# A feed-forward down projection by seven products of halves, with part of its side work on GpSimd and ScalarE and the residual's scale inside the down stage

## The chip, the cores and the metric

The kernel runs on one core of one Trainium2 chip. The metric is the device time of one execution in microseconds (us); the time before is the median of three runs, 1853.4 us (1850.56 to 1854.05).

## The reference

One decoder layer in float32 with 1024 tokens, D_MODEL = 1024 and D_FF = 2816. Two attention branches give h; then comes the feed-forward part, whose last product is what the change is about:

```python
h = _layernorm(alpha * x + attention_branches(x), ...)
ug = _causal_conv3(h @ w_up, conv)          # (1024, 2 * 2816), gate half and value half
f = silu(ug[..., :2816]) * ug[..., 2816:]   # (1024, 2816)
out = _layernorm(alpha * h + f @ w_down, ln2_g, ln2_b)   # w_down is (2816, 1024)
```

(The helper names of these lines are shortened here; the shapes and the order are the reference's.)

## The kernel before

**Precision.** Every float32 operand of TensorE is kept as a high part (a copy rounded to the format that TensorE takes at full pace) and a low part (operand minus high part). A product of a 128-row block is three matmuls, high x high, low x high, high x low, which `split3` issues (L1055, L1056, L1057). So each operand costs one copy (ScalarE or GpSimd) and one subtraction (VectorE or GpSimd), and TensorE gets three matmuls of 128 x 512.

**Engines and order.** The program is one straight instruction list per engine, written by hand; semaphores join them. SyncE (SP) issues most of the transfers, ScalarE a few. An engine that waits holds up all that stands behind it in its list, SP's transfers too.

**The up stage** computes the transposed u = (h @ w_up), two f row blocks (a pair) at a time, so there are 11 pairs. The four halves of a pair's weights and of h are multiplied by a seven-product scheme (Strassen's, in Winograd's form): seven products of halves in place of eight, at the price of sums of the operands and of the results. There are two such sets for a pair (gate and value blocks), 14 products of 12 matmuls each. Their weights pass through a ring of 8 slots: ScalarE makes the high part (`up_high`, L2777) when TensorE has freed the slot, GpSimd the low part (`up_low`, L990), and some weight sums on the way. When a pair's products are done, ScalarE reads banks back: copies of a bank into `p_sb` (L2810, L2816), the first tap of the convolution for the gate (`gate_id`, L2826, into `up_g`) and for the value, and silu. VectorE adds the other taps (L2130, L2135) and multiplies silu(gate) by the value in `value_conv` (L2153), which leaves f in `up_g`: two row blocks, each in two halves of 512 tokens. SP stores each half to `d_f` in DRAM as soon as `f_ok` counts it (`f_store`, L787). `gate_id` of the next pair overwrites `up_g`, and so waits until the stores have landed (`f_out`).

**The down stage** computes tokens x D_MODEL: `down(i, t)` for 22 weight slots i (11 for each half of the output's columns), 8 token tiles t, two row blocks of f and three matmuls each, 6 matmuls of 128 x 512 a call into one of eight banks. f comes back from DRAM in row blocks of 1024 tokens (`f_load`, L790, eight buffers `f_raw`); ScalarE makes the high part (`f_high`, L2927), VectorE the low part (`f_low`, L1576), and each f block is fetched and split twice, once for each column half. Weights: GpSimd makes both parts in one pass each (L928, L930). The rows of h for the residual are fetched whole by ScalarE's queue (L2981) into `z_tok`, VectorE applies the first layer norm's gain and bias to them, and alpha enters when a bank is evicted (`scalar_tensor_tensor` of z_tok, alpha and the bank, L2250). Then the second layer norm follows row by row: statistics on VectorE, the scaling on ScalarE, the gain on VectorE (L2256), the bias on GpSimd (L1043), the stores on SP (L841) and ScalarE.

## Time and the profile before

| | before |
|---|---|
| three runs, median | 1853.4 us |
| profiled execution | 1850.84 us |
| its span | 1849.0 us |
| TensorE matmuls busy | 1783.6 us (96%) |
| TensorE weight loads busy | 1484.4 us (80%) |
| VectorE busy | 906.2 us (49%) |
| ScalarE busy | 719.3 us (39%) |
| GpSimd busy | 917.0 us (50%) |
| granted TensorE clock | 0.993 of full |
| HBM read, written | 159.14 MB, 58.74 MB |

The profiled execution is one run with the profiler on; its span runs from the first to the last recorded instruction. Records of matmuls overlap, so the mean length of a record isn't the time that one matmul adds; a count over a stretch gives that. Busy shares are means over stages with different limits.

### The profile page before, as it was taken

The page shows a single profiled execution, that of the slowest core. Times are in us where ns is not written, and L with a number is a line of the kernel's source. Part 1 is how long each engine was busy: PE and PEld are TensorE (multiplying, and loading weights), DVE is VectorE, ACT ScalarE, POOL GpSimd, SP SyncE. Part 2 cuts the span into 40 slices and gives each one's busy share as a digit, 9 for nine tenths or more (in the row PEclk, how much of TensorE's full clock was granted, in tenths as well). Part 3 has the DMA queues.
Part 4 walks back from the last instruction along what each step waited for, and adds up shares of the span by engine and source line. Part 5 has one row for each costly group of instructions (what it writes and reads, how often), then busy time and mean ns, then how long its engine had stood idle before and what let it go on. Part 6 is the DMA issues. An engine that isn't in the chain of part 4 may idle for free.

```text
span 1849.0 us, 23075 instructions
## 1 busy us (share of the span) xinstructions
PE 1783.6 (96%) x8596; PEld 1484.4 (80%) x8596; DVE 906.2 (49%) x1515; ACT 719.3 (39%) x1295; POOL 917.0 (50%) x718
## 2 busy tenths in 40 slices
PE   8999999999999999999989999999999999999996
PEld 6788887888888777888867888778888888788884
DVE  6213312535444475545455535655455554656447
ACT  6434434333433224545451113744444544211222
POOL 6788754211212542323323375777677766343343
PEclk9999999999999999999999999999999999999998
DMA  5434324213122569223334343223222322754432
GB/s 171 122 103 125 108 88 149 72 55 86 52 92 69 165 208 299 87 80 97 97 114 141 133 182 132 74 85 99 83 77 73 99 80 70 265 190 169 160 103 91
DMA packets 202525, 219.39 MB, mean 119 GB/s; under 512 B 22381, under 2 KB 145437, under 8 KB 202413
## 3 DMA queue, kind: packets, MB, share of 16 engines
q1 hardware_dynamic: 164350, 144.76, 25.3%
q10 hardware_dynamic: 38064, 73.15, 11.2%
q8 instruction: 70, 1.15, 0.3%
q14 instruction: 41, 0.34, 0.1%
HBM read 159.14 MB, written 58.74 MB: 118 GB/s over the span
## 4 chain that ended last, share of the span: by engine, by line
PE 85%; DVE 5%; POOL 3%; ACT 2%; DMA 2%; issue 2%; SPq 1%; ACTq 0%; DVEq 0%; POOLq 0%
PE psum_all L1055 24%; PE psum_all L1057 24%; PE psum_all L1056 24%; PE psum_all L1376 1%; PE psum_all L1392 1%; PE psum_all L1394 1%; PE psum_all L1393 1%; DMA ga_st<-d_sga 1%; DVE pT_lo L1576 1%; PE psum_all L1119 1%; PE psum_all L1123 1%; POOL xs L867 1%; PE psum_all L1090 1%; PE psum_all L1121 1%; PE psum_all L1364 1%
## 5 line engine op out<-in xcount | busy, mean ns | idle before, releaser
L928 POOL CAST w_hi<-w_raw 128x512 fp32r<-128x512 f32 (+4 forms) x104 | 93.1, 895 | 495.2 <-PE psum_all L1057 462.4
L930 POOL TENSOR_TENSOR w_lo<-w_raw,w_hi 128x512 fp32r<-128x512 f32 (+4 forms) x104 | 213.2, 2050 | 8.5
L1055 PE MATMUL psum_all<-xT_hi,w_hi 128*128 128x512 f32 (+1 forms) x456 | 182.3, 400 | 7.5 <-POOL w_lo L864 3.3
L1057 PE MATMUL psum_all<-xT_hi,w_lo 128*128 128x512 f32 (+1 forms) x456 | 179.1, 393 | 0.0
L1056 PE MATMUL psum_all<-xT_lo,w_hi 128*128 128x512 f32 (+1 forms) x456 | 179.1, 393 | 0.0
L1055 PE MATMUL psum_all<-t_hi,w_hi 128*128 128x512 f32 x352 | 137.3, 390 | 2.8 <-DVE psum_all L2190 2.3
L1057 PE MATMUL psum_all<-t_hi,w_lo 128*128 128x512 f32 x352 | 137.0, 389 | 0.0
L1056 PE MATMUL psum_all<-t_lo,w_hi 128*128 128x512 f32 x352 | 137.0, 389 | 0.0
L990 POOL TENSOR_TENSOR w_lo<-s_sb,w_hi 128x512 fp32r<-128x512 f32 x88 | 112.8, 1294 | 43.9 <-ACT w_hi L2777 43.9
L944 POOL TENSOR_SCALAR p_sb<-p_sb,small 128x128 f32<-128x128 f32 (+3 forms) x64 | 48.0, 751 | 171.6 <-DVE small L1954 171.5
L990 POOL TENSOR_TENSOR w_lo<-w_raw,w_hi 128x512 fp32r<-128x512 f32 x66 | 84.8, 1287 | 57.9 <-ACT w_hi L2777 57.7
L1055 PEld LDWEIGHTS psum_all<-xT_hi,w_hi 128*128 128x128 f32 (+1 forms) x456 | 86.5, 190 | 29.2 <-DVE xr L1588 3.5
L1055 PE MATMUL psum_all<-b_hi,w_hi 128*128 128x512 f32 x264 | 104.2, 395 | 3.2 <-ACT p_sb L2810 3.2
L1056 PE MATMUL psum_all<-b_lo,w_hi 128*128 128x512 f32 x264 | 103.9, 394 | 0.0
L1057 PE MATMUL psum_all<-b_hi,w_lo 128*128 128x512 f32 x264 | 103.8, 393 | 0.0
L1057 PEld LDWEIGHTS psum_all<-xT_hi,w_lo 128*128 128x128 f32 (+1 forms) x456 | 86.0, 189 | 19.3
L1056 PEld LDWEIGHTS psum_all<-xT_lo,w_hi 128*128 128x128 f32 (+1 forms) x456 | 86.1, 189 | 17.8
L864 POOL TENSOR_TENSOR w_lo<-w_raw,w_hi 128x512 fp32r<-128x512 f32 x56 | 73.1, 1313 | 44.9 <-ACT w_hi L2289 44.9
L1055 PE MATMUL psum_all<-x_h,w_hi 128*128 128x512 f32 x224 | 87.4, 390 | 1.6 <-POOL w_lo L864 0.8
L1682 DVE TENSOR_TENSOR xp<-psum_all,xp 128x512 f32<-128x512 f32 x14 | 9.7, 690 | 160.8 <-PE psum_all L1057 160.8
L1057 PE MATMUL psum_all<-x_h,w_lo 128*128 128x512 f32 x224 | 87.2, 389 | 0.0
L1056 PE MATMUL psum_all<-x_l,w_hi 128*128 128x512 f32 x224 | 87.2, 389 | 0.0
(536 smaller groups left out, 4873.0 us busy)
## 6 DMA issues: line engine op xcount, KB each, us to landing
w_raw<-in_w_up_dram SPq DMA_DIRECT2D x44, 512.0 KB, 4.1
f_raw<-d_f SPq DMA_DIRECT2D x44, 512.0 KB, 3.5
w_raw<-in_w_in_dram SPq DMA_DIRECT2D x36, 512.0 KB, 4.7
d_f<-up_g SPq DMA_DIRECT2D x44, 256.0 KB, 3.2
w_raw<-in_w_down_dram SPq DMA_DIRECT2D x22, 512.0 KB, 4.5
w_raw<-in_w_out_dram SPq DMA_DIRECT2D x8, 1024.0 KB, 5.1
x_tok<-in_x_dram SPq DMA_DIRECT2D x8, 512.0 KB, 6.7
d_sga<-x_st ACTq DMA_DIRECT2D x16, 256.0 KB, 2.0
```

The source lines that it names most:

```text
L864: nc.gpsimd.tensor_tensor(x_ring(g, True), x_operand(g), x_ring(g).bitcast(F32), ALU.subtract).then_inc(sm["up_w"], 1)
L867: nc.gpsimd.tensor_tensor(dst, a, b, op).then_inc(sm["s_ok"], 1)
L928: wc.done(nc.gpsimd.tensor_copy(w_hi[b][:, w], src[:, w]))
L930: low = nc.gpsimd.tensor_tensor(w_lo[b][:, w], src[:, w], w_hi[b][:, w].bitcast(F32), ALU.subtract)
L944: nc.gpsimd.tensor_scalar(p_sb[s % 3][:, 0:wp], p_sb[s % 3][:, 0:wp], prec[:, s % 2:s % 2 + 1], 1.0, ALU.mult, ALU.mult).then_inc(sm["p_no ...
L990: nc.gpsimd.tensor_tensor(ring(g, True), operand(g), ring(g).bitcast(F32), ALU.subtract).then_inc(sm["up_w"], 1)
L1055: pe.matmul(out_ap, ah, bh, start=start and i == 0, stop=False, skip_group_check=more)
L1056: pe.matmul(out_ap, ah, bl, start=False, stop=False, skip_group_check=more)
L1057: last = pe.matmul(out_ap, al, bh, start=False, stop=stop and i == len(terms) - 1, skip_group_check=more)
L1090: last = pe.transpose(bank(kind)[:, i * P:(i + 1) * P], s_ap, ident[:, :])
L1119: pe.matmul(psum[5][:, 0:DV], att[i % 2][:, :], v_tok[:, t, :], start=True, stop=t == 0)
L1121: pe.matmul(psum[5][:, 0:DV], q_all[h % 2][:, t, 0:2, :], state[:, :], start=False, stop=True)
```

## The change

The down stage takes the seven-product scheme too. f is cut into blocks by row block (even or odd one of a pair) and by token half, w_down likewise by row block and by column half (`NEAR`, `FAR`). There are 77 steps g, seven products p of 11 steps m; a step multiplies one f tile of 128 x 512 (four token tiles) by one weight tile of 128 x 512, three matmuls for each token tile.

- **f and its sums.** After a pair's last f half, VectorE forms three sums of the pair's four f halves, and replaces one half by a difference (`f_sums`). SP then stores seven tiles (`f_store`), after all of the sums. The down stage fetches one tile of 128 x 512 a step (`fa_load`, five buffers), so that each is fetched once.
- **Weights.** The whole of w_down is fetched as four blocks of 2816 KB, one of them in two transfers, and stays in SBUF: one block before the end of the up stage, two at its end, the last ahead of the f tile of step 10. The high parts come from ScalarE (`wd_high`), the low parts from GpSimd (`up_low`), through the ring of the up stage. Three of the four weight sums are on VectorE ("t1", "t2", "t4" in `dn_sums`), one on GpSimd.
- **Results.** ScalarE copies the first product's banks to three places of z each and the fourth's to one (`first_rows`); VectorE adds the others (`evict`). Where products share a bank, the matmuls accumulate in it.
- **Residual.** SP fetches half rows of h into two buffers (`h_load`), two steps ahead of their use; VectorE applies gain and bias and adds alpha times the row to z ("h" in `dn_sums`), in steps 24 to 26, 31 to 39 and 54 to 57.
- **End.** The last six steps are done token tile by token tile. In the last layer norm GpSimd now multiplies by the gain as well as adding the bias for the first four rows, and adds the bias for two more.

```diff
-        d_f = dram("d_f", [FT, P, S])
+        d_f = dram("d_f", [7, FT // 2, P, HALF])
...
+        for m in range(NK):
+            dn_at(7 + m // 2, "t1", m)
+        for m in range(NK):
+            dn_at(10 + m if m < 2 else 12 + m, "t2", m)
+        for j in range(16):
+            dn_at(24 + j if j < 3 else 28 + j if j < 12 else 42 + j, "h", j)
+        for t in range(4):
+            dn_at(27 + t, "S2", t)
+            dn_at(49 + t, "S3", t)
+            dn_at(60 + t, "S1", t)
+        for m in range(NK):
+            dn_at(42 + m, "t4", m)
...
-                sp.dma_start(d_f[2 * m + u, :, half * HALF:(half + 1) * HALF], up_g[u][half][:, :]).then_inc(f_out[u], 16)
...
+            def f_store(m):
+                sp.wait_ge(sm["f_sums"], m + 1)
+                for what, src, landed in (("A11", up_g[0][0], f_out[0]), ("S3", up_g[0][1], f_out[0]), ("A12", up_g[1][0], f_out[1]),
+                                          ("A22", up_g[1][1], f_out[1]), ("S1", f_sum[0], s_out), ("S2", f_sum[1], s_out), ("S4", f_sum[2], s_out)):
+                    sp.dma_start(d_f[DN.index(what), m], src[:, :]).then_inc(landed, 16)
...
+            def fa_load(g):
+                if g >= AR:
+                    sp.wait_ge(sm["fs_lo"], g - AR + 1)
+                p, m = divmod(g, NK)
+                sp.dma_start(fa_raw[g % AR][:, :], d_f[p, m]).then_inc(tile_in[g % AR], 16)
+
+            def h_load(j):
+                if j >= 2:
+                    sp.wait_ge(*dn_sum("h", j - 2))
+                t, c = H_ROWS[j]
+                sp.dma_start(hr[j % 2][:, :], d_h[t * P:(t + 1) * P, c]).then_inc(hr_in[j % 2], 16)
...
-                    for u in range(2):
-                        for half in range(2):
-                            f_store(m - 1, u, half)
+                    f_store(m - 1)
...
+            for g in range(AR):
+                fa_load(g)
+            sp.wait_ge(sm["up_mm"], DN0)
+            sp.dma_start(wd_all[1][:, :, :], wdq[0][:, :, FAR]).then_inc(wd12_in[0], 16)
+            sp.dma_start(wd_all[3][:, :, :], wdq[1][:, 0:8, FAR]).then_inc(wd22_in[0], 16)
+            sp.dma_start(wd_all[4][:, :, :], wdq[1][:, 8:NK, FAR]).then_inc(wd22_in[0], 16)
+            for g in range(AR, DN_STEPS):
+                if g == 8:
+                    f_store(PAIRS - 1)
+                if g == NK - 1:
                     for u in range(2):
-                        for half in (1, 0):
-                            f_store(PAIRS - 1, u, half)
...
+                        sp.wait_ge(f_out[u], 32 * PAIRS)
+                    sp.wait_ge(s_out, s_out_from + 48 * PAIRS)
+                    sp.dma_start(wd_all[2][:, :, :], wdq[1][:, :, NEAR]).then_inc(wd21_in[0], 16)
+                    sp.wait_ge(sm["h_stored"], 16 * TT)
+                fa_load(g)
+                for j in range(16):
+                    if ("h", j) in DN_AT.get(g + 2, ()):
+                        h_load(j)
...
+            for g in range(DN_STEPS):
+                up_low(PRODUCTS + g)
+                if 13 <= g <= 33 and g % 2:
+                    m = (g - 13) // 2
+                    pool.wait_ge(*wd22_in)
+                    pool.wait_ge(*dn_sum("t1", m))
+                    w_sum(wd12[m], wd22[m][:, :], wd12[m][:, :], ALU.subtract)
...
+                ms.done(nc.gpsimd.tensor_tensor(z[4 + n][:, :], z[4 + n][:, :], ln2_gt[:, :], ALU.mult))
+                ms.wait()
+                nc.gpsimd.tensor_tensor(z[4 + n][:, :], z[4 + n][:, :], ln2_bt[:, :], ALU.add).then_inc(sm["ln2_ok"], 1)
...
+            for t in range(4):
+                for g in range(DN_STEPS - AL, DN_STEPS):
+                    down(g, t)
...
+            def fa_low(g):
+                ve.wait_ge(sm["fs_hi"], g + 1)
+                split_lo(fa[g % AL][1][:, :], fa_raw[g % AR][:, :], fa[g % AL][0][:, :]).then_inc(sm["fs_lo"], 1)
...
+            def f_sums(m):
+                ve.wait_ge(sm["f_ok"], 4 * m + 4)
...
+                (a11, a21), (a12, a22) = up_g
+                vc.done(V.tensor_tensor(f_sum[0][:, :], a21[:, :], a22[:, :], ALU.add))
+                vc.wait()
+                vc.done(V.tensor_tensor(f_sum[1][:, :], f_sum[0][:, :], a11[:, :], ALU.subtract))
+                vc.wait()
+                vc.done(V.tensor_tensor(f_sum[2][:, :], a12[:, :], f_sum[1][:, :], ALU.subtract))
+                V.tensor_tensor(a21[:, :], a11[:, :], a21[:, :], ALU.subtract).then_inc(sm["f_sums"], 1)
...
+                    f_sums(m)
...
+            f_sums(PAIRS - 1)
...
+                    ve.wait_ge(sm["up_w"], DN0 + m + 1)
+                    ve.wait_ge(*wd12_in)
+                    V.tensor_tensor(wd11[m][:, :], wd12[m][:, :], wd11[m][:, :], ALU.subtract).then_inc(sm["u_sum"], 1)
+                if what == "t2":
+                    if m == 0:
+                        ve.wait_ge(*wd22_in)
+                    ve.wait_ge(*dn_sum("t1", m))
+                    ve.wait_ge(sm["up_w"], DN0 + NK + m - 1 if m >= 2 else DN0)
+                    V.tensor_tensor(wt2[m % 2][:, :], wd22[m][:, :], wd11[m][:, :], ALU.subtract).then_inc(sm["u_sum"], 1)
+                if what == "t4":
+                    ve.wait_ge(sm["up_w"], DN0 + 2 * NK + m + 1)
+                    op(V.tensor_tensor(wd21[m][:, :], wd21[m][:, :], wd11[m][:, :], ALU.add))
+                    V.tensor_tensor(wd21[m][:, :], wd21[m][:, :], wd22[m][:, :], ALU.subtract).then_inc(sm["u_sum"], 1)
...
+                    ve.wait_ge(hr_in[m % 2], hr_from + 16 * (m // 2 + 1))
+                    op(V.tensor_tensor(row, row, ln1_gt[:, c], ALU.mult))
+                    op(V.tensor_tensor(row, row, ln1_bt[:, c], ALU.add))
+                    ve.wait_ge(sm["snap"], SNAP0 + (12 if m < 12 else 16))
+                    V.scalar_tensor_tensor(z[t][:, c], row, ALPHA, z[t][:, c], ALU.mult, ALU.add).then_inc(sm["u_sum"], 1)
+                    ve.wait_ge(*made)
...
+            def fa_high(g):
+                ac.wait_ge(sm["up_mm"], DN0 + (g - AL + 1 if g >= AL else -6))
+                ac.wait_ge(tile_in[g % AR], 16 * (g // AR + 2))
+                A.copy(fa[g % AL][0][:, :], fa_raw[g % AR][:, :]).then_inc(sm["fs_hi"], 1)
+
+            def wd_high(g):
+                p, m = divmod(g, NK)
+                ac.wait_ge(sm["up_mm"], DN0 + g - 7)
+                ac.wait_ge(*(wd11_in, dn_sum("t2", m), wd21_in, (sm["s_ok"], 8 * (XPAIRS + PAIRS) + m + 1),
+                             dn_sum("t1", m), dn_sum("t4", m), wd22_in)[p])
+                A.copy(ring(PRODUCTS + g), dn_w(g)).then_inc(sm["up_hi"], 1)
...
+            def first_rows(what, t):
+                p = DN.index(what)
+                ac.wait_ge(sm["up_mm"], DN0 + (p + 1) * NK)
+                for row, c in (((t, FAR), (4 + t, NEAR), (4 + t, FAR)) if what == "A11" else ((t, NEAR),)):
+                    A.copy(z[row][:, c], psum[DN_X[t]]).then_inc(sm["snap"], 1)
...
+            for g in range(4, DN_STEPS + 2):
+                if g < DN_STEPS:
+                    fa_high(g)
+                if g >= 6:
+                    wd_high(g - 2)
```

**First place: SP, the middle of the down stage.** Before, f blocks and weight slots alternate, and each waits for its own buffer to be free.

```order
L790 DMA f_raw_308<-d_f 128x1024 [waits fs_lo]
L790 DMA f_raw_309<-d_f 128x1024 [waits fs_lo]
L691 DMA w_raw_50<-in_w_down_dram 128x2x512 [waits w_split]
L790 DMA f_raw_310<-d_f 128x1024 [waits fs_lo]
L790 DMA f_raw_311<-d_f 128x1024 [waits fs_lo]
L691 DMA w_raw_49<-in_w_down_dram 128x2x512 [waits w_split]
L790 DMA f_raw_304<-d_f 128x1024 [waits fs_lo]
```

After, at steps 27 to 31: `fa_raw_308` to `fa_raw_312` are the five buffers of f tiles, `hr_327` and `hr_328` the two of half rows of h; `u_sum` counts VectorE's sums, the use of a row of h among them.

```order
L831 DMA fa_raw_310<-d_f 128x512 [waits fs_lo]
L831 DMA fa_raw_311<-d_f 128x512 [waits fs_lo]
L831 DMA fa_raw_312<-d_f 128x512 [waits fs_lo]
L837 DMA hr_328<-d_h 128x512 [waits u_sum]
L831 DMA fa_raw_308<-d_f 128x512 [waits fs_lo]
L837 DMA hr_327<-d_h 128x512 [waits u_sum]
L831 DMA fa_raw_309<-d_f 128x512 [waits fs_lo]
```

Between two f tiles there is now a row of h with a wait of its own, for VectorE's use of the row two before.

**Second place: ScalarE, the first steps of the down stage.** Before, an f block's copies alternate with the fetch of a row of h, and no weight passes through ScalarE.

```order
L2981 DMA z_tok<-d_h 128x1024
L2927 CAST f_0h<-f_raw_308 128x1024 [waits tile_in4,fs_lo,w_used]
L2927 CAST f_1h<-f_raw_309 128x1024 [waits tile_in5]
L2981 DMA z_tok<-d_h 128x1024
L2927 CAST f_2h<-f_raw_310 128x1024 [waits tile_in6,fs_lo,w_used]
L2927 CAST f_3h<-f_raw_311 128x1024 [waits tile_in7]
L2981 DMA z_tok<-d_h 128x1024
```

After, beginning with step 4: `fa4h` is the high part of step 4's f tile, `fa5h`, `fa0h`, `fa1h`, ... those of steps 5, 6, 7, ...; `wd_303` holds the first product's weights, `w_hi_51` and `w_hi_52` are the ring. The first of these weight copies is that of step 4.

```order
L3052 CAST fa4h<-fa_raw_312 128x512 [waits tile_in4,up_mm]
L3052 CAST fa5h<-fa_raw_308 128x512 [waits tile_in0,up_mm]
L3052 CAST fa0h<-fa_raw_309 128x512 [waits tile_in1,up_mm]
L3059 CAST w_hi_51<-wd_303 128x512 [waits tile_in5,up_mm]
L3052 CAST fa1h<-fa_raw_310 128x512 [waits tile_in2,up_mm]
L3059 CAST w_hi_51<-wd_303 128x512 [waits tile_in5,up_mm]
L3052 CAST fa2h<-fa_raw_311 128x512 [waits tile_in3,up_mm]
L3059 CAST w_hi_52<-wd_303 128x512 [waits tile_in5,up_mm]
L3130 DMA ln_gain<-in_ln_g_dram 128x1024
```

A weight copy of step g-2 now stands behind the copy of the f tile of step g.

**Third place: VectorE, the end of a pair in the up stage.** Before, the last f half (L2153) is followed at once by the taps of the next pair's gate.

```order
L2135 SCALAR_TENSOR_TENSOR psum_all<-psum_all,cw,up_v_285 128x512 [waits vs]
L2153 TENSOR_TENSOR up_g_283<-up_g_283,psum_all 128x512 [waits g_si,vs,v_c]
L2130 SCALAR_TENSOR_TENSOR up_g_280<-psum_all,cw,up_g_280 128x511 [waits g_id]
L2135 SCALAR_TENSOR_TENSOR up_g_280<-psum_all,cw,up_g_280 128x510 [waits vs]
L2130 SCALAR_TENSOR_TENSOR up_g_282<-psum_all,cw,up_g_282 128x511 [waits g_id]
```

After (the same lines have moved to L2186, L2191 and L2209): `up_g_280` to `up_g_283` are the four halves, `f_sum_337` to `f_sum_339` the three sums.

```order
L2191 SCALAR_TENSOR_TENSOR psum_all<-psum_all,cw,up_v_285 128x512 [waits vs]
L2209 TENSOR_TENSOR up_g_283<-up_g_283,psum_all 128x512 [waits g_si,vs,v_c]
L2259 TENSOR_TENSOR f_sum_337<-up_g_281,up_g_283 128x512 [waits lat_out,f_ok]
L2261 TENSOR_TENSOR f_sum_338<-f_sum_337,up_g_280 128x512 [waits vs]
L2263 TENSOR_TENSOR f_sum_339<-up_g_282,f_sum_338 128x512 [waits vs]
L2264 TENSOR_TENSOR up_g_281<-up_g_280,up_g_281 128x512
L2186 SCALAR_TENSOR_TENSOR up_g_280<-psum_all,cw,up_g_280 128x511 [waits g_id]
L2191 SCALAR_TENSOR_TENSOR up_g_280<-psum_all,cw,up_g_280 128x510 [waits vs]
L2186 SCALAR_TENSOR_TENSOR up_g_282<-psum_all,cw,up_g_282 128x511 [waits g_id]
```

Four sums stand between the last f half and the next pair's taps. On SP, the four stores that each waited for their own half (`f_ok`) have become seven in a row that follow the last sum (`f_sums`). On TensorE the order has 132 matmuls fewer.

## Rows read from the trace of the kernel before

**Rows 1.** The page, busy time (share of the span) and instructions of each engine.

```profile
PE 1783.6 (96%) x8596; PEld 1484.4 (80%) x8596; DVE 906.2 (49%) x1515; ACT 719.3 (39%) x1295; POOL 917.0 (50%) x718
```

**Rows 2.** Stretches: busy PE, PEld, DVE, ACT, POOL (count), clock, DMA share, GB/s.

```profile
1400.00:1420.00 20.00, 20.00 (x90) 16.55 (x89) 7.23 (x11) 9.04 (x16) 10.65 (x9) 1.00 0.39 126
1500.00:1600.00 100.00, 95.76 (x421) 78.49 (x420) 61.96 (x94) 43.07 (x68) 58.85 (x44) 1.00 0.40 144
1600.00:1700.00 100.00, 100.00 (x443) 82.81 (x442) 55.37 (x32) 18.04 (x18) 39.33 (x18) 1.00 0.54 182
```

**Rows 3.** ScalarE in order of time, 1442 to 1451: start, length, idle before and releaser.

```profile
1442.60 0.62 ACT L2777 CAST w_hi<-s_sb 128x512 fp32r<-128x512 f32 x1 [1.61 <-PE psum_all L1057]
1443.13 0.77 ACT L2826 ACTIVATE up_g<-psum_all,cw 128x512 f32<-128x512 f32 x1
...
1448.04 0.62 ACT L2777 CAST w_hi<-w_raw 128x512 fp32r<-128x512 f32 x1 [0.90 <-PE psum_all L1057]
1448.57 0.58 ACT L2816 COPY p_sb<-psum_all 128x512 f32<-128x512 f32 x1
...
1450.76 0.62 ACT L2777 CAST w_hi<-w_raw 128x512 fp32r<-128x512 f32 x1 [1.08 <-PE psum_all L1057]
```

**Rows 4.** What TensorE waited for, 1500 to 1849: us in total, times, longest.

```profile
PE psum_all L1055 <- POOL w_lo L930: 4.3, 2, 2.3
PE psum_all L1055 <- DVE psum_all L2190: 2.3, 1, 2.3
```

**Rows 5.** VectorE in order of time, 1441 to 1446, over the same pair's end.

```profile
1441.87 0.69 DVE L2153 TENSOR_TENSOR up_g<-up_g,psum_all 128x512 f32<-128x512 f32 x1
1443.93 0.75 DVE L2130 SCALAR_TENSOR_TENSOR up_g<-psum_all,cw,up_g 128x511 f32<-128x511 f32 x1 [1.38 <-ACT up_g L2826]
1444.72 0.75 DVE L2135 SCALAR_TENSOR_TENSOR up_g<-psum_all,cw,up_g 128x510 f32<-128x510 f32 x1
```

**Rows 6.** The store of that f half (L787), 1442 to 1444: issue, and landing.

```profile
L787 SPq DMA_DIRECT2D d_f<-up_g x1: 319/319/319, 1442.6 to 1442.6; - x1
...
DMA to landing us min/median/max: 2.0/2.0/2.0
```

**Rows 7.** VectorE in order of time, 1701 to 1709: low parts of f.

```profile
1701.59 1.23 DVE L1576 TENSOR_TENSOR f_2l<-f_raw,f_2h 128x1024 fp32r<-128x1024 f32 x1 [3.92 <-ACT f_2h L2927]
1702.73 3.42 DVE L1576 TENSOR_TENSOR f_3l<-f_raw,f_3h 128x1024 fp32r<-128x1024 f32 x1
```

**Rows 8.** GpSimd over the same time: the low part of a weight slot.

```profile
1701.73 3.34 POOL L930 TENSOR_TENSOR w_lo<-w_raw,w_hi 128x1024 fp32r<-128x1024 f32 x1
```

**Rows 9.** Groups of GpSimd, 1400 to 1500: count, busy, mean ns, idle before.

```profile
L990 POOL TENSOR_TENSOR w_lo<-w_raw,w_hi 128x512 fp32r<-128x512 f32 x17 | 21.9, 1286 | 18.1 <-ACT w_hi L2777 18.1
```

**Rows 10.** The first eight loads of f (L790), 1567 to 1572: issues and landings.

```profile
L790 SPq DMA_DIRECT2D f_raw<-d_f x8: 394/436/648, 1568.0 to 1571.5; - x8
...
DMA to landing us min/median/max: 5.5/9.3/12.0
```

**Rows 11.** The tile sgb_st: loads of 128 x 512 on ScalarE's queue.

```profile
L2666 ACTq DMA_DIRECT2D sgb_st<-d_sgb x16: 326/326/453, 984.7 to 1053.2; - x16
...
DMA to landing us min/median/max: 2.6/2.8/6.4
```

**Rows 12.** TensorE in order of time, its last matmul.

```profile
1833.23 0.39 PE L1057 MATMUL psum_all<-w_hi,f_last1l 128*128 128x512 f32 x1
```

**Rows 13.** VectorE in order of time, the last eviction.

```profile
1838.35 0.68 DVE L2250 SCALAR_TENSOR_TENSOR z_tok<-z_tok,psum_all 128x512 f32<-128x512 f32 x1
```

**Rows 14.** GpSimd in order of time, the last bias.

```profile
1838.19 2.36 POOL L1043 TENSOR_TENSOR z_tok<-z_tok,ln_bias 128x1024 f32<-128x1024 f32 x1 [1.16 <-DVE z_tok L2256]
```

**Rows 15.** TensorE in order of time, 1205 to 1212: a wait and the matmuls behind.

```profile
1209.47 0.50 PE L1055 MATMUL psum_all<-b_hi,w_hi 128*128 128x512 f32 x1 [3.17 <-ACT p_sb L2810]
...
1211.03 0.63 PE L1057 MATMUL psum_all<-b_hi,w_lo 128*128 128x512 f32 x1
1211.46 0.63 PE L1055 MATMUL psum_all<-b_hi,w_hi 128*128 128x512 f32 x1
```

345 lines of the change are left out of this document (187 added, 158 removed).

## The prediction

> **What bounds the kernel now.** I read the busy line of the page, then the stretches, then who waits for whom. TensorE is busy for 96% of the span [rows 1]. In the up stage a stretch of 20 us is filled by 90 matmuls, in the down stage 100 us by 443: about 0.226 us each, though every single record lasts longer because they overlap [rows 2]. ScalarE's copies of up weights, released by TensorE one product at a time, come 2.72 us apart (1448.04, 1450.76) [rows 3]. A product is 12 matmuls, so one costs 0.2267 us. From 1500 us on TensorE waits three times, 6.6 us in all [rows 4]. So TensorE's count of matmuls sets the time, and work on the other engines is free as long as it keeps its lead. The question is whether the new side work keeps it.
>
> **What is removed.** Down had 22 x 8 x 6 = 1056 matmuls; seven products of 11 steps, 4 token tiles and 3 terms have 924. 132 x 0.2267 = **-29.9 us**. The three waits of rows 4 (two for weight parts made in one piece by GpSimd, one for a low part that held up VectorE) are for things that no longer exist in that form: **-6.6**.
>
> **The hand-over between pairs of the up stage.** Today the last product of a pair's f is formed by VectorE at 1441.87, ends at 1442.56 [rows 5], is stored at once and lands 2.0 us later [rows 6]. ScalarE writes the next pair's gate over it at 1443.13, copies the fifth product's bank at 1448.57 until 1449.15, and TensorE wants that bank at 1450.76 (the beat that releases the next copy) [rows 3]: a lead of 1.6 us. Now four sums come after 1442.56, and only then seven stores. The sums read two SBUF tiles each. In rows 7 such an operation of 1024 columns takes 1.23 us, but 3.42 us when GpSimd's pass is running, and it ends 1.08 us after that pass does (1701.73 + 3.34 = 1705.07, then 1706.15) [rows 7, 8]: the two take turns. GpSimd's 1.29 us low part [rows 9] starts near 1443.3, behind the first sum. So: first sum until 1443.4, GpSimd until 1444.65, three more sums of 0.6 to 0.7 until 1446.5. First store lands at 1448.5. Eight loads issued back to back put 512 KB down each (12.0 + 1571.5 - 5.5 - 1568.0) / 7 = 1.4 us [rows 10], so 256 KB take 0.7, and the second store, which ScalarE's gate pass waits for, lands at 1449.2. Behind it in ScalarE's order stand a weight copy, the other gate pass and the first silu, which waits for two VectorE passes (0.78 each, rows 5), then another copy, and then the copy of the bank: 1449.2 + 0.77 + 1.6 + 0.6 + 0.5 = 1452.8, done 1453.4. That is 2.6 us late, ten times: **+26**. Below: without the turns at the port 1.5 each, 15; above: stores behind a weight load, 4 each, 40.
>
> **Start of the down stage.** At the end of up (call it 0) SP issues 5632 KB of weights, and f tiles 5 to 7 only after them. 22 x 0.7 + 2.0 = 17.4; f6 at 18.8. ScalarE copies f6 ahead of the weights of step 4 (second place under the change), so these come at 18.8 + 0.6 + 0.6 + 1.3 = 21.3, and TensorE wants step 4 at 4 x 2.72 = 10.9: 10.4 us. Seven stores and then 2816 KB more stand ahead of f8 and f10, which by the same count costs another 5: **+15**. Below, 5, if the weights come at the first stage's pace only in part; above, 20.
>
> **The residual's rows.** This is the largest term. SP fetches a half row of h two steps ahead, into two buffers. At its step g it first waits until VectorE has used row j-2, and for j = 5 to 11 that use is in VectorE's step g itself. f tile g+1 stands behind this wait in SP's order (first place under the change). So from step 31 to 37 nothing is fetched ahead. One round is: row and f tile issued together; a half row alone lands in 2.6 us at least, the second 0.7 behind it [rows 10, 11], 3.3; ScalarE's copy 0.67; low part 0.72; GpSimd's turn 1.25; mult, add and scaled add 2.2: 8.1 us, against 2.72 for TensorE. 7 x 5.4 = 38; TensorE waits for the weights that ScalarE copies behind the f tile. The lead (VectorE at most five steps ahead, weights three) takes off up to 8 if it is whole, but steps 24 to 26 use it: **+37** (30 to 41). Step 24 has one such round, **+5**; steps 54 and 55 have two, after sums that used up the lead, **+11**.
>
> **The port elsewhere.** In steps 14 to 22 each step needs, taking turns, 1.29 for GpSimd's low part, 0.65 for its weight sum every other step, 0.69 + 0.69 on VectorE: 3.3 us in 2.72. In steps 42 to 52 it is 1.29 + 0.69 + 1.4 = 3.4. Together 5.4 + 7.5 over, of which the lead hides part: **+8** (0 to 13). Rows 7 and 8 show the taking of turns for 1024 columns and low parts only; I take it for all passes with two SBUF inputs. The Trainium skill, SBUF — State Buffer (section "SBUF: two separate sides"), says more than the rows: the pair of ports shared by VectorE and GpSimd is an exclusive lock held for a whole instruction, for any VectorE operation with two SBUF inputs. By that page the sum is my forecast; if only the forms in the rows were bound, it would be the first rival.
>
> **The end.** Today TensorE's last matmul starts at 1833.23, the last eviction at 1838.35, because VectorE is 4.7 us behind [rows 12, 13]; the span ends 15.4 us after the last matmul. Now a token tile takes 18 matmuls, 4.1 us, and VectorE keeps up. But GpSimd multiplies and adds four tiles and adds two more, ten passes of 2.36 us [rows 14], from about 6 us into the last 19 us of matmuls: it ends 12 us behind TensorE, and three last stores follow: +5. ScalarE normalizes ahead of the last two weight copies: +2. **+7** (0 to 10).
>
> **The clock.** After an idle of 3.17 us the matmuls start 0.43 us apart (1211.03, 1211.46) in place of 0.23, the 1.2 GHz level [rows 15]. The waits of 2.3 us did not do this: the stretch they lie in has the clock at 1.00, 2.4 GHz [rows 2, 4]. The long waits here will; while TensorE is starved it costs nothing, at two or three other places 1.6: **+4**.
>
> Sum: -29.9 - 6.6 + 26 + 15 + 37 + 5 + 11 + 8 + 7 + 4 = +76.5. The profiled execution took 1850.8, the median of the runs is 1853.4; 1850.8 + 76.5 = 1927, and with half of the 2.6 between them, 1929.
>
> **Rivals.**
> 1. *The port costs nothing at 512 columns, and the lead is whole.* Hand-over 15, start 15, rounds of 6.9 us in steps 31 to 37 with the lead off 18, steps 54 and 55 3, end 2, clock 4: -36.5 + 57 = 1871. For it: the shown case is 1024 wide. Against: the same kind of unit, and GpSimd's low part falls in every step. 0.2.
> 2. *The lead hides the waits (the other side).* f tiles five steps ahead are 13.6 us of cover. If the row fetch delays SP by less than 13.6 / 7 + 2.72 = 4.7 us per round, it costs nothing, and if the stores land within the 1.6 us of the hand-over that is free too: -36.5 + 15 = 1829. The point that decides is the round: 4.7 us or less. Against: the fetch alone takes 3.3 and VectorE's part 2.9. 0.04.
> 3. *The clock stays low.* If TensorE is kept at 1.2 GHz through most starved stretches, the last round and each hand-over pay too: 10 x 1.6 + 5 more, 1950. For it: waits of 2.6 are near the 3.17 that did it. 0.1.
> 4. *The change removes no TensorE time*, since weights as moving operands cost more. Against: shape and count per step are as before, and the order shows 132 fewer. 0.01; it would give 1960.
>
> The forecast itself has 0.65 (1900 to 1955). Within 0.2%, which is about what a measurement of this kernel can tell from no change, lie hardly any: 0.02. Range 1868 to 1955: down to rival 1 and up to the edge of the forecast; about 2 in 10 lie outside, from rivals 2 and 3 and the lower half of rival 1.
>
> **What would show it.** PE waits in the up stage: ten of about 2.6 us, ended by ScalarE's copy to p_sb. Waits of 5 us or more in the down stage, on low parts of weights, at steps 4, 24, 31 to 37 and 54. On SP, row loads that wait for VectorE with an f tile issued right behind. VectorE passes with two SBUF inputs well over 0.69 us. The span after the last matmul near 20 us. Wrong if f tiles land early in steps 31 to 37, or if VectorE's sums keep to 0.69 us.

## The result, and the profile after

The changed kernel takes 1941.64 us (median of 4 runs, 1940.45 to 1945.71), the kernel before 1852.24 us on the same chip: 1.0489 times as long, with an interval of 1.0469 to 1.0509. That is 89.4 us more. The forecast was 1929, the range 1868 to 1955. The profiled execution has a span of 1944.0 us, 95.0 more than before.

The page of the changed kernel, busy time and then two of the rows of 40 slices (busy tenths of TensorE, tenths of its clock), to set beside [rows 1]:

```profile
PE 1792.5 (92%) x8464; PEld 1480.8 (76%) x8464; DVE 1026.8 (53%) x1668; ACT 767.5 (39%) x1421; POOL 968.1 (50%) x766
...
PE   8999999999999999999889998989999987876985
...
PEclk9999999999999999999999999999999998986998
```

TensorE's records are 132 fewer, but its busy time is 9 us more, since matmuls last longer at a lower clock. The new gaps of the down stage stand in the last seven slices; those of the up stage are too short to show in a slice of 48.6 us. What TensorE waited for from 1200 us on (total, times, longest), to set beside [rows 4]:

```profile
PE psum_all L1107 <- POOL w_lo L1031: 57.8, 14, 10.5
PE psum_all L1107 <- ACT p_sb L2942: 26.3, 10, 3.0
...
PE psum_all L1107 <- issue: 2.8, 2, 2.4
PE psum_all L1107 <- DVE psum_all L2246: 2.0, 1, 2.0
PE psum_all L1107 <- DVE up_g L2226: 0.6, 1, 0.6
```

Two rows say nearly everything: ten waits at the hand-over between pairs, ended by ScalarE's copy into `p_sb`, and fourteen in the down stage, ended by the low part of a weight tile. (The 2.4 us under "issue" are the wait of step 33, one of the same row of seven; four waits under 1 us make 2.4 us more.) The single waits at steps 4, 8, 23, then 30 and 36 (the first and the last of the row of seven), 53 and 54 of the down stage:

```profile
1647.05 0.77 PE L1107 MATMUL psum_all<-w_hi,fa4h 128*128 128x512 f32 x1 [10.52 <-POOL w_lo L1031]
...
1666.75 0.77 PE L1107 MATMUL psum_all<-w_hi,fa2h 128*128 128x512 f32 x1 [6.37 <-POOL w_lo L1031]
...
1713.66 0.76 PE L1107 MATMUL psum_all<-w_hi,fa5h 128*128 128x512 f32 x1 [3.29 <-POOL w_lo L1031]
...
1741.63 0.76 PE L1107 MATMUL psum_all<-w_hi,fa0h 128*128 128x512 f32 x1 [7.15 <-POOL w_lo L1031]
...
1792.90 0.77 PE L1107 MATMUL psum_all<-w_hi,fa0h 128*128 128x512 f32 x1 [3.81 <-POOL w_lo L1031]
...
1848.28 0.76 PE L1107 MATMUL psum_all<-w_hi,fa5h 128*128 128x512 f32 x1 [6.27 <-POOL w_lo L1031]
...
1856.98 0.77 PE L1107 MATMUL psum_all<-w_hi,fa0h 128*128 128x512 f32 x1 [3.49 <-POOL w_lo L1031]
```

**The hand-over.** VectorE at the end of a pair, in order of time:

```profile
1423.34 0.69 DVE L2209 TENSOR_TENSOR up_g<-up_g,psum_all 128x512 f32<-128x512 f32 x1
1424.06 0.69 DVE L2259 TENSOR_TENSOR f_sum<-up_g,up_g 128x512 f32<-128x512 f32 x1
1424.78 1.83 DVE L2261 TENSOR_TENSOR f_sum<-f_sum,up_g 128x512 f32<-128x512 f32 x1
1426.64 0.69 DVE L2263 TENSOR_TENSOR f_sum<-up_g,f_sum 128x512 f32<-128x512 f32 x1
1427.25 0.68 DVE L2264 TENSOR_TENSOR up_g<-up_g,up_g 128x512 f32<-128x512 f32 x1
```

GpSimd at the same time, and behind it ScalarE's gate pass and its copy of the bank:

```profile
1424.77 1.28 POOL L1031 TENSOR_TENSOR w_lo<-s_sb,w_hi 128x512 fp32r<-128x512 f32 x1 [1.43 <-ACT w_hi L2903]
```

```profile
1430.85 0.78 ACT L2952 ACTIVATE up_g<-psum_all,cw 128x512 f32<-128x512 f32 x1 [6.15 <-DMA d_f<-up_g]
...
1434.27 0.58 ACT L2942 COPY p_sb<-psum_all 128x512 f32<-128x512 f32 x1
```

The last f half ends at 1424.03. The second sum meets GpSimd's pass, begins with it and lasts 1.83 us: 1.28 for GpSimd and 0.55 of its own remainder. The sums end at 1427.93, the stores are issued, ScalarE's gate pass starts 6.8 us after the last f half (before: 0.57, [rows 3, 5]), and the bank is copied 3.4 us later.

**A round of steps 30 to 36.** The timeline of all engines from SP's row load to the next one, with most rows of TensorE left out:

```profile
1752.51 0.32 SPq L837 DMA_DIRECT2D hr<-d_h  x1
...
1752.87 0.43 SPq L831 DMA_DIRECT2D fa_raw<-d_f  x1
...
1755.96 0.62 ACT L3052 CAST fa4h<-fa_raw 128x512 fp32r<-128x512 f32 x1 [7.84 <-DMA fa_raw<-d_f]
1756.48 0.61 ACT L3059 CAST w_hi<-wd 128x512 fp32r<-128x512 f32 x1
1756.68 0.69 DVE L1632 TENSOR_TENSOR fa4l<-fa_raw,fa4h 128x512 fp32r<-128x512 f32 x1 [4.20 <-ACT fa4h L3052]
1757.17 1.32 POOL L1031 TENSOR_TENSOR w_lo<-wd,w_hi 128x512 fp32r<-128x512 f32 x1 [5.97 <-ACT w_hi L3059]
1757.29 1.75 DVE L2327 TENSOR_TENSOR hr<-hr,ln_gain 128x512 f32<-128x512 f32 x1
...
1758.64 0.77 PE L1107 MATMUL psum_all<-w_hi,fa2h 128*128 128x512 f32 x1 [4.39 <-POOL w_lo L1031]
...
1759.07 0.69 DVE L2328 TENSOR_TENSOR hr<-hr,ln_bias 128x512 f32<-128x512 f32 x1
...
1759.80 0.69 DVE L2330 SCALAR_TENSOR_TENSOR z<-hr,z 128x512 f32<-128x512 f32 x1
...
1760.52 0.32 SPq L837 DMA_DIRECT2D hr<-d_h  x1
```

Nothing is ahead of anything: row and f tile are issued together when VectorE has used a row, land 3 us later, are copied, split and used, and the next pair is issued. Four such issues lie at 1752.51, 1760.52, 1769.41 and 1777.99, 8.5 us apart. TensorE waits at each step for the weight tile that ScalarE copies behind the f tile. The seven waits of steps 30 to 36 make 28.5 us.

By stages of the two profiled executions (first to last matmul of a stage, all in us):

| | before | after | difference |
|---|---|---|---|
| up to the first seven-product pair | 1209.5 | 1214.2 | +4.7 |
| up stage, to the first matmul of down | 379.7 | 410.4 | +30.7 |
| down stage, to the last matmul | 244.1 | 298.8 | +54.7 |
| after the last matmul | 15.8 | 20.6 | +4.8 |

The first +4.7 lies ahead of everything that the change touches. In the profiled executions below this point lies anywhere between 1205.5 and 1214.5, so it says nothing of the change.

### The profile page after: what moved, and what is told of

It is laid out like the page before. It is cut to its first block, busy times and chain, and to the rows that moved or that the text cites. A ratio compares the mean times of both kernels' runs of the same rounds, so it can differ in the third digit from the quotient of the medians.

```text
span 1944.0 us, 23352 instructions
## 1 busy us (share of the span) xinstructions
PE 1792.5 (92%) x8464; PEld 1480.8 (76%) x8464; DVE 1026.8 (53%) x1668; ACT 767.5 (39%) x1421; POOL 968.1 (50%) x766
## 4 chain that ended last, share of the span: by engine, by line
PE 61%; DVE 18%; DMA 8%; ACT 4%; issue 4%; POOL 4%; SPq 1%; ACTq 0%; POOLq 0%; DVEq 0%
PE psum_all L1107 17%; PE psum_all L1109 16%; PE psum_all L1108 16%; DMA fa_raw<-d_f 3%; DVE up_v L2186 1%; DVE psum_all L2191 1%; DVE up_g L2209 1%; DMA d_f<-up_g 1%; DVE hr L2327 1%; DMA ga_st<-d_sga 1%; PE psum_all L1444 1%; PE psum_all L1428 1%; PE psum_all L1445 1%; PE psum_all L1446 1%; DVE hr L2328 1%
## 5 line engine op out<-in xcount | busy, mean ns | idle before, releaser
L969 POOL CAST w_hi<-w_raw 128x512 fp32r<-128x512 f32 (+3 forms) x82 | 66.7, 813 | 347.7 <-PE psum_all L1109 339.0
L1031 POOL TENSOR_TENSOR w_lo<-wd,w_hi 128x512 fp32r<-128x512 f32 x55 | 81.9, 1500 | 155.2 <-ACT w_hi L3059 155.2
L971 POOL TENSOR_TENSOR w_lo<-w_raw,w_hi 128x512 fp32r<-128x512 f32 (+3 forms) x82 | 144.5, 1762 | 6.7
L1107 PE MATMUL psum_all<-b_hi,w_hi 128*128 128x512 f32 x264 | 105.6, 400 | 29.5 <-ACT p_sb L2942 26.3
L1031 POOL TENSOR_TENSOR w_lo<-w_raw,w_hi 128x512 fp32r<-128x512 f32 x66 | 84.8, 1288 | 41.1 <-ACT w_hi L2903 41.0
L1109 PEld LDWEIGHTS psum_all<-xT_hi,w_lo 128*128 128x128 f32 (+1 forms) x456 | 87.1, 191 | 19.7
## 6 DMA issues: line engine op xcount, KB each, us to landing
wd<-in_w_down_dram SPq DMA_DIRECT2D x3, 2816.0 KB, 11.4
```

Of the source, the lines that this page charges most:

```text
L969: wc.done(nc.gpsimd.tensor_copy(w_hi[b][:, w], src[:, w]))
L971: low = nc.gpsimd.tensor_tensor(w_lo[b][:, w], src[:, w], w_hi[b][:, w].bitcast(F32), ALU.subtract)
L1031: nc.gpsimd.tensor_tensor(ring(g, True), operand(g), ring(g).bitcast(F32), ALU.subtract).then_inc(sm["up_w"], 1)
L1107: pe.matmul(out_ap, ah, bh, start=start and i == 0, stop=False, skip_group_check=more)
L1109: last = pe.matmul(out_ap, al, bh, start=False, stop=stop and i == len(terms) - 1, skip_group_check=more)
```

## The experiments

Twelve kernels ran. The kernel before took 1853 to 1854 us beside them. This table sums them up (median; ratio to the kernel before with its interval; stages as above):

| kernel | us | ratio | up | down | end |
|---|---|---|---|---|---|
| changed kernel | 1941.6 | 1.0489 (1.0469 to 1.0509) | 410.4 | 298.8 | 20.6 |
| four row buffers | 1894.5 | 1.0213 (1.0192 to 1.0234) | 417.1 | 251.6 | 20.7 |
| rows behind later f tiles | 1897.2 | 1.0248 (1.0223 to 1.0274) | 412.0 | 252.3 | 20.7 |
| stores ahead of the sums | 1917.1 | 1.0336 (1.0312 to 1.0361) | 382.9 | 301.9 | 20.7 |
| weights ahead on ScalarE | 1954.4 | 1.0540 (1.0513 to 1.0567) | 413.6 | 310.7 | 19.2 |
| order of the first loads | 1942.6 | 1.0476 (1.0453 to 1.0499) | 411.8 | 296.0 | 20.7 |
| GpSimd's low parts cut | 1898.3 | 1.0246 (1.0231 to 1.0261) | 399.0 | 268.0 | 20.6 |
| stores ahead, new start | 1901.8 | 1.0267 (1.0251 to 1.0282) | 381.1 | 287.3 | 20.6 |
| stores, start and four row buffers: the three repairs | 1854.5 | 1.0011 (0.9998 to 1.0023) | 383.4 | 239.3 | 20.7 |
| three repairs, gain on VectorE | 1848.1 | 0.9972 (0.9961 to 0.9982) | 384.6 | 238.9 | 14.5 |
| that, rows spread | 1848.2 | 0.9976 (0.9964 to 0.9987) | 384.3 | 236.2 | 15.9 |
| that (rows not spread), low parts on VectorE | 1841.1 | 0.9934 (0.9915 to 0.9953) | 383.0 | 232.2 | 14.2 |
| that, rows spread and low parts on VectorE | 1839.2 | 0.9921 (0.9905 to 0.9937) | 383.5 | 230.0 | 14.2 |

**Four row buffers.**

```diff
-        hr = [put("hr0", ...), put("hr1", ...)]
+        hr = [put("hr0", ...), put("hr1", ...), wt2[0], wt2[1]]
...
-                    sp.wait_ge(*dn_sum("h", j - 2))
+                    sp.wait_ge(*dn_sum("h", j - 4))
```

> The changed kernel with four buffers for the half rows of h in place of two (the two that held the second product's weight sums, free by then), so that SP's load of row j waits for the use of row j-4. Theory (SP's wait for VectorE's use of the row two before holds back the f tile behind it): the rounds of steps 30 to 36, which took 8.5 us each with 34.2 us of waits and further matmuls at the lower clock, fall to VectorE's own work in a step, about 0.7 + 1.75 + 1.2 + 0.7 = 4.35 us against 2.72, nine times 1.6 = 14.7 us, nearly all of which the lead of five steps (13.6) takes up. The waits at steps 23, 53 and 54 (3.4, 6.4 and 3.7) shrink to half. About 1890 us (1880 to 1900). Rival (VectorE's work with its turns at the port is the bound itself, the fetch is not): the rounds keep to 7 us or more, 1925 us or more.

1894.5 us, inside the theory's range. The rounds are gone; in the down stage 25.1 us of waits for weight parts are left of 57.8, 17 of them at the start, and none from step 30 on is over 3.2 us. Some 5 us of waits for the low parts of f tiles are new. The rival, 1925 us or more, is out. (The 34.2 us of waits that the text gives for steps 30 to 36 are 28.5 us by the trace of the changed kernel; the rest of the loss there was slow matmuls.)

**Two row buffers, but the wait behind later f tiles.**

```diff
-                    if ("h", j) in DN_AT.get(g + 2, ()):
+                    if ("h", j) in DN_AT.get(g - 2, ()):
```

> The changed kernel with its two row buffers, where SP issues the load of the row for step s behind the f tile of step s+2 and not behind that of step s-2, so that three more f tiles stand ahead of its wait for VectorE. Theory (what costs is the place of the wait in SP's order, with f tiles behind it): the same as four buffers give, 1894 us (1888 to 1901), since a row's load of 3 us fits in VectorE's own 4.35 us a step. Rival (two buffers are too few whatever the order): the rounds stay over 6 us, 1920 us or more.

1897.2 us. The row's wait now stands behind four more f tiles (those of steps s-1 to s+2 for a row of step s), and this one line does what two more buffers do, within the intervals. So the number of buffers was not what cost, but where the wait for one stood. SP now issues row and f tile every 3.8 us, the pace of VectorE's own work in a step; VectorE is busy for 7.4 of the 7.6 us between the first and the last of these issues:

```profile
1738.22 0.32 SPq L837 DMA_DIRECT2D hr<-d_h  x1
...
1742.09 0.32 SPq L837 DMA_DIRECT2D hr<-d_h  x1
...
1745.85 0.32 SPq L837 DMA_DIRECT2D hr<-d_h  x1
```

**Stores ahead of the sums.** The difference goes to a fourth sum buffer, so the three plain halves (k = 0 to 2 of a pair's seven stores) can leave at once:

```diff
-                sp.wait_ge(sm["f_sums"], m + 1)
...
+                    if k == 3:
+                        sp.wait_ge(sm["f_sums"], m + 1)
+                    if k < 3:
+                        sp.wait_ge(sm["f_ok"], 4 * m + (1 if m < PAIRS - 1 else 2, 3 if m < PAIRS - 1 else 4, 4)[k])
...
-                    ac.wait_ge(f_out[u], 32 * m)
+                    ac.wait_ge(sm["f_sums"], m)
+                    ac.wait_ge(f_out[u], (16 + 16 * u) * m)
```

> The changed kernel with a fourth sum buffer, so that the difference of f halves is not made in place, and the plain halves are stored as soon as each is there; the next pair's gate pass then waits for these stores and for the sums, not for stores behind the sums. Theory (sums, then stores in a row, stand ahead of ScalarE's gate pass): the gate pass starts some 2.7 us earlier, the ten waits of 2.6 us for the copy of the fifth product's bank fall under 0.4 each, 24 us less: 1917 us (1912 to 1921). Rival (the sums alone, with GpSimd's turns between them, are late enough): ten waits of 1.2 us or more remain, 1928 us.

1917.1 us, the theory's figure. Of the ten waits for `p_sb` the list has one left, of 0.2 us, and the up stage takes 382.9 us, 27.5 less. The sums themselves are still there, turns included; they fit.

**Weights ahead of f tiles on ScalarE.**

```diff
-                if g < DN_STEPS:
-                    fa_high(g)
                 if g >= 6:
                     wd_high(g - 2)
+                if g < DN_STEPS:
+                    fa_high(g)
```

> The changed kernel with one swap on ScalarE: in each step of the down stage the copy of the weights of step g-2 goes ahead of the copy of the f tile of step g. Theory (weights that are long in SBUF wait behind an f tile that isn't there yet): TensorE goes on for two steps (5.4 us) at each stall before it lacks the f tile itself. The two stalls of the start lose about 6 together, that of step 23 its 3.4, those of 30 to 36 and of 53 and 54 lose 5.4 each, and the rounds themselves keep their 8 us: 1922 us (1914 to 1928). Rival (the f tile is wanted at the same time as the weights, so order decides nothing): within 3 us of 1941.

1954.4 us, 13 us slower, where theory and rival both had no loss: this theory fell. At the start it gained next to nothing (step 4 begins 22.1 us into the stage, in the changed kernel 22.5), because tile 5 still stood ahead of the weights of step 4, and tile 5 is behind the weight blocks too. In the second product, whose weights are sums made by VectorE, it closed a circle. ScalarE in that stretch, then VectorE:

```profile
1686.89 0.62 ACT L3059 CAST w_hi<-wt 128x512 fp32r<-128x512 f32 x1 [1.74 <-DVE wt L2317]
1687.41 0.61 ACT L3052 CAST fa0h<-fa_raw 128x512 fp32r<-128x512 f32 x1
```

```profile
1688.06 1.34 DVE L1632 TENSOR_TENSOR fa0l<-fa_raw,fa0h 128x512 fp32r<-128x512 f32 x1 [1.26 <-ACT fa0h L3052]
```

The weight copy waits for VectorE's sum, the f copy stands behind it, and VectorE waits 1.26 us for the f copy before it can go to its next sum. In the changed kernel the f copy is early enough there. TensorE has new short waits from step 14 on (1.3 us at steps 16, 18 and 20), and waits of 4.6 and 2.3 us at steps 24 and 27. That VectorE arrives at the rows of h with its lead used up is the reading that fits; no run tests it.

**The order of the first loads.**

```diff
+            for g in (5, 6, 7, 8):
+                fa_load(g)
             sp.dma_start(wd_all[1][:, :, :], wdq[0][:, :, FAR]).then_inc(wd12_in[0], 16)
+            fa_load(9)
+            f_store(PAIRS - 1)
...
+                if g in (14, 16, 18):
+                    c = slice(2 * (g - 14), min(2 * (g - 14) + 4, NK))
+                    sp.dma_start(wd_all[2][:, c, :], wdq[1][:, c, NEAR]).then_inc(wd21_in[0], 16)
```

> The changed kernel with another order of SP's transfers at the start of the down stage: f tiles 5 to 8 ahead of the second weight block, the last pair's stores and f tiles 9 to 11 behind it, then the third block, and the fourth in three pieces between later f tiles. Theory (f tiles queue behind 5.6 MB and then 2.8 MB of weights): the waits of 10.7 us at step 4 and 6.5 at step 8 give way to a few of 2 to 3, some 10 us less: 1931 us (1926 to 1935). Rival (the bytes have to come in any case and the transfers share the bandwidth, so the waits only move): 1938 us or more.

1942.6 us: no change, the rival's figure, but not for the rival's reason. f tile 5 landed in 2.7 us and its copy began at 1629.11, so the weights of step 4 came early, but now the low part of f tile 4 was late: it began 16.4 us into the stage (1642.56), in the changed kernel 11.9 us into it (1636.47). VectorE at that time:

```profile
1636.86 0.69 DVE L2264 TENSOR_TENSOR f_sum<-up_g,up_g 128x512 f32<-128x512 f32 x1
1637.58 1.68 DVE L2266 TENSOR_TENSOR f_sum<-f_sum,up_g 128x512 f32<-128x512 f32 x1
1639.29 1.67 DVE L2268 TENSOR_TENSOR f_sum<-up_g,f_sum 128x512 f32<-128x512 f32 x1
1640.89 1.75 DVE L2269 TENSOR_TENSOR up_g<-up_g,up_g 128x512 f32<-128x512 f32 x1
1642.56 0.68 DVE L1637 TENSOR_TENSOR fa4l<-fa_raw,fa4h 128x512 fp32r<-128x512 f32 x1
```

In VectorE's list the low part of tile 4 stands behind the last pair's convolutions and its four sums, and three of these met GpSimd, which had weights earlier than before; in the changed kernel the same four sums lasted 0.69 us each. Step 4 began 17.2 us into the stage in place of 22.5, so the second limit lay 5.3 us behind the first. The last pair's stores and tiles 9 and 10 were then late in their turn, which cost a wait of 6.3 us at step 10. In the two profiles the down stage is 2.8 us shorter and the up stage 1.4 us longer, the latter with two slow stretches behind hand-over waits that the changed kernel's profile lacks; of the 10 us of the theory at most that 2.8 was there.

**A new start.** f tiles 5 to 8 ahead of the second weight block and the fourth block in pieces, as just now, but tile 10 ahead of the third block; the last pair's plain half stored by itself; the low parts of tiles 4 to 6 between the convolutions; the weight tiles up to step 10 ahead of their f tiles on ScalarE; all on top of the kernel with early stores. VectorE's part:

```diff
             end_conv_first(0)
+            fa_low(4)
             end_conv_main(1)
+            fa_low(5)
             end_conv_seam(1)
             end_conv_first(1)
+            fa_low(6)
```

> The kernel with stores ahead of the sums (1917 us) and a new start of the down stage in three parts: on SP f tiles 5 to 8 ahead of the second weight block, the last pair's plain f half stored by itself and its tile 10 fetched ahead of the third block, the fourth block in three pieces later; on VectorE the low parts of tiles 4 to 6 between the last pair's convolutions, not behind them; on ScalarE the first eleven weight tiles each ahead of its f tile. Theory (transfers were one limit of the start and VectorE's list the next): the two waits of 10.7 and 6.5 us leave about 4 in all: 1903 us (1897 to 1909). Rival (VectorE has simply too much to do there, whatever the order): 1911 us or more.

1901.8 us, 15.3 less than with early stores alone, as expected. The waits of 10.9 and 6.6 us at steps 4 and 8 are gone; one of 4.0 us at step 2, ended by VectorE's pass on the last pair's `up_g`, is there in place of 0.6. What each part of the new start gave was not run by itself. With the four row buffers too:

> The one before with the four row buffers too. Theory (the causes add up): 1903 - 47 = 1856 us (1850 to 1864), near the kernel before with its 1854: the 36.5 us that the change saves TensorE are eaten by what is left, VectorE's turns with GpSimd in the down stage and the longer end. Rival (with one stall gone, the shared port holds up the next step anyway): 1870 us or more.

1854.5 us. The three repairs give 87.1 us together, against 47.1 + 24.5 + 15.3 = 86.9 (the first two each by itself, the third on top of the second): the causes add up.

**GpSimd's low parts cut.** From the second pair on GpSimd makes 2 of 512 columns of each; the rest is stale, so part of the computation is left out.

```diff
-                nc.gpsimd.tensor_tensor(ring(g, True), operand(g), ...)
+                c = slice(0, 2 if g >= 14 else HALF)
+                nc.gpsimd.tensor_tensor(ring(g, True)[:, c], operand(g)[:, c], ...)
```

> The changed kernel with GpSimd's weight low parts from the second pair of the up stage on cut to 2 of 512 columns, so that GpSimd's passes are nearly gone; the rest of each low part keeps stale data, so this leaves part of the computation out. Theory (VectorE's passes with two SBUF inputs and GpSimd's take turns, and this is part of each stall): VectorE's f sums and its passes on the rows of h last 0.69 us each. The ten waits at the hand-over fall from 2.6 to about 1.4 us (12 less), the rounds of steps 30 to 36 from 8.5 to about 7.1 (9 less), the waits at 23, 53 and 54 nearly vanish (11 less), and those of the start lose 1.3 each for the low part itself: about 1906 us (1896 to 1916). Rival (the turns cost nothing that TensorE sees): 1936 us or more.

1898.3 us, 43 less (the theory's middle was 35), 11.4 of it in the up stage and 30.8 in the down stage. VectorE's passes that met GpSimd before, second sum and multiplication by the gain (min/median/max in ns):

```profile
L2262 DVE TENSOR_TENSOR f_sum<-f_sum,up_g x11: 691/725/726, 1211.3 to 1615.7; 128x512 f32<-128x512 f32 x11
```

```profile
L2328 DVE TENSOR_TENSOR hr<-hr,ln_gain x16: 680/685/694, 1681.6 to 1811.6; 128x512 f32<-128x512 f32 x16
```

In the changed kernel the medians were 1816 and 1750 ns. Nothing was changed on VectorE. The ten waits at the hand-over went from 26.3 to 17.3 us. These end with ScalarE's copy of a bank, so they show the turns alone; in the down stage the cut also takes GpSimd's own 1.3 us from in front of TensorE, and the run doesn't tell the two apart there.

**The end, and the low parts on VectorE.** On top of the three repairs, VectorE multiplies the first four rows by the gain (`end_gain`); then also the rows of h are spread over more steps, or the low parts of steps 24 to 57 go to VectorE (`w_low`), or both.

```diff
-                ms.done(nc.gpsimd.tensor_tensor(z[4 + n][:, :], z[4 + n][:, :], ln2_gt[:, :], ALU.mult))
...
+            def end_gain(n):
+                row = (4 + n) % TT
+                ve.wait_ge(sm["ln2_n"], n + 1)
+                V.tensor_tensor(z[row][:, :], z[row][:, :], ln2_gt[:, :], ALU.mult).then_inc(sm["ln2_g"], 1)
...
-            dn_at(24 + j if j < 3 else 28 + j if j < 12 else 42 + j, "h", j)
+            dn_at(24 + 3 * j // 2 if j < 12 else 54 + 3 * (j - 12) // 2, "h", j)
...
+        LOW0, LOW1 = 24, 58
...
+                if LOW0 <= g - 2 < LOW1:
+                    w_low(g - 2)
```

> The version with all three repairs (1854.5 us), where in the last layer norm VectorE multiplies the first four rows by the gain, as the kernel before did, and GpSimd only adds biases. Theory (the longer end is GpSimd's ten passes of 2.4 us and the turns that they force on VectorE): the span after the last matmul falls from 20.5 to about 16 us: 1850 us (1848 to 1852). Rival (the last row's chain is what ends last, whoever multiplies the others): within 1 us of 1854.5.

> The same with the twelve rows of h spread over steps 24 to 40, two in three steps, and the last four over 54 to 58. Theory (VectorE and GpSimd together are full at the port, not at single steps: about 229 us of such passes in a down stage of about 209 us of matmuls): spreading hides a little more, 2 to 4 us: 1847 us (1844 to 1850). Rival (the crowd in neighbouring steps is the whole of what is left): 1842 us or less.

> The version with four repairs, rows not spread, where VectorE makes the weight low parts of steps 24 to 57 (0.69 us each) in place of GpSimd (1.29 each). Theory (the two engines' passes with SBUF inputs take turns, so that moving 34 of them to the engine that is faster at it frees 34 x 0.6 = 20 us of the shared port): VectorE's passes there last 0.69 us, and of the 17 us of waits from step 24 on some 8 to 10 go, low clock with them: 1841 us (1836 to 1846). Rival (VectorE is then simply overloaded, with 34 x 0.69 = 23 us more to do): 1852 us or more.

> Both edits, rows spread and low parts of steps 24 to 57 on VectorE. Theory: VectorE's work in a step is then about 2.9 us against 2.72 and the lead covers the rest: 1837 us (1833 to 1842), faster than the kernel before by 0.9%. Rival (overloaded VectorE): 1850 us or more.

1848.1, 1848.2, 1841.1 and 1839.2 us. The gain on VectorE shortens the end to 14.5 us, and the kernel is now faster than before by 0.28%. Spreading the rows gives nothing by itself: 1848.2 lies in the range of the theory, but the 2 to 4 us less that it spoke of are not there (1848.1 without), and the rival's 1842 is out. The low parts on VectorE give 7 us more. The stretch 1650 to 1750 of the kernel without them, then of the one with them (busy PE, PEld, DVE, ACT, POOL; clock, DMA share, GB/s):

```profile
1650.00:1750.00 100.00, 91.52 (x388) 73.01 (x387) 98.05 (x87) 40.44 (x74) 67.01 (x42) 0.98 0.33 109
```

```profile
1650.00:1750.00 100.00, 93.66 (x401) 75.22 (x400) 98.02 (x133) 40.73 (x73) 21.62 (x13) 0.98 0.41 127
```

VectorE is at 98% in both, but in the first it does 87 passes in that time and in the second 133: a large part of its busy time was time in which it stood behind GpSimd. Its new low parts last

```profile
L1647 DVE TENSOR_TENSOR w_lo<-wd,w_hi 128x512 fp32r<-128x512 f32 x29 | 20.9, 721 | 0.0
```

0.72 us each, against 1.29 on GpSimd [rows 9]. So the weight part is itself 0.57 us sooner, and the other passes have fewer turns to wait for; the run has both at once and doesn't part them.

## Why the prediction was right, step by step

**Fewer matmuls, -29.9.** Right. The stages at full clock run at the pace of [rows 2], and what the down stage lost is accounted for below with 924 x 0.2267 = 209.5 us as its base.

**Three waits gone, -6.6.** Two of the three went. The third, for a bank in the last pair (2.3 us in [rows 4], on L2190), is still there on its moved line, 2.0 us on L2246. The prediction laid it to a low part of f and called it gone with the old form; the name in the row is `psum_all`, a pass that adds `p_sb` to a bank, and VectorE's list of that stretch, two low parts of f ahead of it included, is the same in both kernels. 2.0 us too good.

**The hand-over, +26.** Right in mechanism and size: ten waits, 26.3 us. The gate pass began 6.8 us after the last f half, where 1449.2 - 1442.56 = 6.6 was worked out, and the turns came as forecast (GpSimd's pass with the second sum, nothing between the others). Without turns 15 was the lower bound; the cut low parts left 17.3. What a wait costs is a little more than the idle time that the profile gives for it: without a wait a pair takes 38.1 us (168 x 0.2267), with one of 2.6 to 2.7 us 41.0 to 41.1. That makes some 3 us over ten pairs, and is most of what the up stage has over the 26; 1.5 more stand under the clock.

**The start, +15.** Measured 10.5 and 6.4 us, 16.9; the mechanism was f tiles behind 5632 KB and then 2816 KB. That it was the only limit was wrong: the order of loads alone gave nothing in the medians and 2.8 us in the down stage of its profile, since VectorE's list held the next.

**The rows, +37, +5 and +11.** The largest term, and right. The rounds were 8.5 us where 8.1 was worked out. From 1734.3, the end of step 29, to 1792.9, the start of step 36, lie 58.6 us for six steps that need 16.3: 42.3 lost, a little over the bound of 41. 28.5 of it were waits (2.4 to 7.2 us each, not 5 or more at every step as the signs had it) and 13.6 matmuls at the lower clock. The extra over 8.1 has two parts: in two of the rounds GpSimd made a weight sum behind its low part, which made VectorE's second pass last 1.66 us too (0.97 more for the round), and from the issue of the row to VectorE's low part passed 4.1 to 4.8 us, where 4.0 was worked out. The single round at step 24 cost 3.3 and the two at 54 and 55 cost 9.8; TensorE stopped one step earlier than numbered in each case.

**The port elsewhere, +8.** Wrong: there is no wait in steps 9 to 22 and 37 to 52. The lead covered it all. (That steps 23 and 53 stop one early because the lead was used up there is argued, not shown.) The passes themselves took turns as said. By count, GpSimd's 88 passes of 1.29 us and VectorE's 169 with two SBUF inputs of 0.69 us make an estimated 230 us of turns in a down stage that has 209.5 us of matmuls. So with the three repairs the down stage could not come down to its matmuls; it took 239.3 us, 4.8 less than before, and the longer end took that back. But the count is a floor and not the whole: moving 34 passes to the engine that is quicker at them takes 20 us off it, to 210, and the down stage went from 238.9 to 232.2 only. Part of the 22.7 us that are left over the matmuls are the waits at steps 2, 11 and 24 (1.9, 5.9 and 3.7 us) and the slow matmuls behind them; no run explains these. The Trainium skill, SBUF — State Buffer (section "SBUF: two separate sides"), says that the pair of ports shared by VectorE and GpSimd is an exclusive lock for a whole instruction, and that a VectorE pass with two SBUF inputs takes it too, against a GpSimd pass that reads SBUF. The runs agree, with 1.83 us against 0.73 for the same sum, and in the changed kernel's trace the 40 passes of L2209, which read a bank, keep to 0.69 us although 31 of them lie over a pass of GpSimd.

**The end, +7.** It was 4.8, and the cause is shown: without GpSimd's multiplications the end is 14.5 us.

**The clock, +4.** The most mis-sized term: 14.6 in the down stage and 1.5 in the up stage. This stretch of the rounds (busy PE, PEld, DVE, ACT, POOL; clock, DMA share, GB/s) has the clock at 0.70:

```profile
1734.09:1792.90 58.81, 30.32 (x74) 20.95 (x73) 27.20 (x28) 9.50 (x18) 12.76 (x10) 0.70 0.23 81
1792.90:1841.62 48.72, 48.72 (x203) 40.15 (x204) 47.93 (x51) 18.37 (x33) 24.05 (x16) 0.94 0.23 76
```

In the first of them, the rounds, matmuls start 0.42 us apart (1752.78, 1753.20), the 1.2 GHz level, but TensorE is starved there and waits for the round in any case. Outside, it costs: the 17 steps from 1792.9 to 1841.85 took 48.95 us without a wait, where 46.2 is the full pace, and each of the six stalls of the down stage (steps 4, 8, 23, the rounds as one, 53, 54) has such a tail, of 1.6 to 2.9 us, 14.0 in all. The down stage's 54.7 are -29.9 - 4.7 (its two waits of before with the time that they left) + 16.9 + 3.3 + 42.3 + 9.8 + 2.4 (four waits under 1 us), and the rest, 14.6, is this. The forecast had counted tails at two or three places; there were six. Some hand-over waits leave a tail too: over the five profiled kernels that have them at full length, 11 of 45 pairs came 42.4 to 42.7 us apart and not 41.1, though none in the changed kernel's own profile.

The prediction also drew a line that the runs don't bear out: the waits of 2.3 us had not lowered the clock before, so only the long ones would. In the changed kernel the hand-over wait of 2.70 us at 1434.90 left the clock at full, and the shorter one of 1.99 us at 1617.41 was followed by matmuls 0.42 us apart (1617.88, 1618.30), 1.5 us lost. The two stretches behind these waits (busy PE, PEld, DVE, ACT, POOL; clock, DMA share, GB/s):

```profile
1434.00:1438.00 4.00, 3.10 (x13) 2.55 (x14) 0.63 (x1) 2.40 (x6) 2.59 (x2) 1.00 0.26 73
1617.40:1621.00 3.60, 3.59 (x9) 2.83 (x10) 3.47 (x6) 2.13 (x4) 0.00 (x0) 0.53 0.00 0
```

The length of a wait alone doesn't tell whether the clock falls.

The profiled execution is 95.0 - 76.5 = 18.5 us above the sum: +10.6 for the clock in the down stage, +5.3 for the rounds, +4.7 in the up stage over the 26, +4.7 ahead of it, +2.4 for the four short waits, +1.9 at the start and +1.9 for the misread wait, less 8 for the port, 1.7 for step 24, 1.2 for 54 and 55 and 2.2 for the end. By the medians the forecast was 12.6 us too low (1929 against 1941.6). The errors partly cancel, the 8 us of the port against the clock above all, and that the figure came out this near is in part luck; the order of the largest terms and the mechanisms of the hand-over, the start, the rounds and the end stood.

One sum of the prediction doesn't come out: the costs listed for the first rival (15, 15, 11 for its rounds, 3, 2 and 4) make 50, not 57, and so 1865 us, 3 below the lower edge of the range. Only that edge hangs on it.

## What to carry to other kernels

A wait in a queue's list is paid by everything behind it, so ask of each new one what stands behind and how far ahead that was; here a line that moved one wait behind four more loads was worth 44 us, nearly as much as doubling the buffers. When work is added to two engines, add up their passes that must take turns over the stage, not each engine's own share: VectorE and GpSimd were busy for 53% and 50% of the span, and their turns in the down stage added up to more than its matmuls. Such a sum is a floor for the stage, not a forecast of it. And when a stall is repaired, look in the trace for what stood just behind it before believing that its whole length comes back.

## What was not expected

- The issue of a transfer itself held SP: of three pieces that make 5632 KB, the last took 6.20 us to issue, the first 0.38, and no wait for a semaphore stands between them. What it waits for no run tells.

```profile
1624.79 0.38 SPq L865 DMA_DIRECT2D wd<-in_w_down_dram  x1
1625.21 0.77 SPq L866 DMA_DIRECT2D wd_near<-in_w_down_dram  x1
1626.03 6.20 SPq L867 DMA_DIRECT2D wd_far<-in_w_down_dram  x1
```

- Stretches that are the same in all kernels differ between executions: the start of the first pair lay between 1205.5 and 1214.5 us, so single profiles say nothing below some 9 us unless stages are compared.
- Why some waits leave a slow tail and others, longer ones among them, don't stays open; no run tells it.
